# A blocked state scan on TensorE: two more products on all four quadrants, with copies that cross the partition halves

## The reference

```python
def step(s, inp):
    r_t, k_t, v_t, kk_t, a_t, w_t = inp
    sa = jnp.einsum("dbhij,dbhj->dbhi", s, kk_t)
    s = (s * w_t[..., None, :] - sa[..., :, None] * (kk_t * a_t)[..., None, :]
         + v_t[..., :, None] * k_t[..., None, :])
    y = jnp.einsum("dbhij,dbhj->dbhi", s, r_t) if readout else None
    return s, y
return lax.scan(step, state0, xs)
```

## Time and profile before

| what | value |
|---|---|
| median of three runs | 1297.73 us (1296.73 to 1299.86) |
| the profiled execution, its own time | 1300.72 us |
| its span, first to last instruction | 1298.9 us |
| PE busy | 1219.1 us (94%) |
| DVE busy | 540.9 us (42%) |
| ACT busy | 360.2 us (28%) |
| POOL busy | 115.3 us (9%) |
| mean granted TensorE clock | 0.982 |
| the scan's loop, steps 1 to 8 | 174.19 to about 368 us of the span |

### The profile page before, as it was taken

One profiled execution on the slowest core, in us unless ns is written; L12 is line 12 of the kernel. 1 busy time (PEld: TensorE's weight loads), 2 busy tenths in 40 slices (PEclk: granted clock), 3 DMA queues, 4 the chain that ended last, 5 costly groups with the idle time before them and its releaser, 6 DMA issues.

```text
span 1298.9 us, 23465 instructions
## 1 busy us (share of the span) xinstructions
PE 1219.1 (94%) x10171; PEld 855.6 (66%) x10171; DVE 540.9 (42%) x1110; ACT 360.2 (28%) x863; POOL 115.3 (9%) x135
## 2 busy tenths in 40 slices
PE   4999889898898999999989999999999979999996
PEld 1435777787777888888868887656678653343333
DVE  3158234446432999970030732575244140111113
ACT  3346144355421321111011211455431032111101
POOL 0004244334100001220000000000000000000000
PEclk9999889999998999999989999999999979999998
DMA  9700013322373334334343333211065539999991
GB/s 389 315 13 33 1 51 117 108 77 76 108 293 130 130 137 185 132 123 171 130 147 141 128 113 136 78 66 65 1 261 195 194 130 373 423 422 420 421 420 76
DMA packets 28038, 225.04 MB, mean 173 GB/s; under 512 B 3424, under 2 KB 6624, under 8 KB 7328
## 3 DMA queue, kind: packets, MB, share of 16 engines
q1 hardware_dynamic: 27536, 222.17, 43.9%
q0 software_dynamic: 256, 1.06, 0.2%
q10 hardware_dynamic: 144, 0.31, 0.1%
HBM read 220.38 MB, written 1.05 MB: 170 GB/s over the span
## 4 chain that ended last, share of the span: by engine, by line
PE 88%; DVE 4%; ACT 3%; issue 2%; DMA 2%; POOL 1%; DVEq 0%; SPq 0%; ACTq 0%
PE ps L738 37%; PE ps L1404 9%; PE ps L1198 6%; PE ps L886 5%; PE ps L1257 5%; PE ps L1455 4%; PE ps L1416 2%; PE ps L1303 2%; PE ps L1274 2%; PE ps L888 2%; PE ps L770 1%; PE ps L1381 1%; PE ps L865 1%; PE ps L1002 1%; PE ps L1288 1%
## 5 line engine op out<-in xcount | busy, mean ns | idle before, releaser
L738 PE MATMUL ps<-mem 128*128 128x256 f32 (+2 forms) x2032 | 499.3, 403 | 9.2 <-DVE mem L2232 4.2
L738 PEld LDWEIGHTS ps<-mem 128*128 128x128 f32 x2032 | 386.7, 192 | 112.2 <-issue 42.7
L2213 DVE SCALAR_TENSOR_TENSOR mem<-ps,mem 128x189 f32<-128x189 f32 (+2 forms) x352 | 148.3, 431 | 15.6 <-ACT mem L1754 4.7
L886 PE MATMUL ps<-mem 64*64 64x64 f32 (+1 forms) x2176 | 106.9, 239 | 19.9 <-DVE mem L2006 3.8
L886 PEld LDWEIGHTS ps<-mem 64*64 64x64 f32 x2176 | 87.9, 138 | 42.7 <-issue 20.7
L1404 PE MATMUL ps<-mem 128*34 128x512 f32 x512 | 112.8, 593 | 0.0
L888 PE MATMUL ps<-mem 64*64 64x64 f32 (+1 forms) x2176 | 105.3, 239 | 2.0 <-issue 1.9
L1516 ACT ACTIVATE mem<-ps 128x512 f32<-128x512 f32 (+4 forms) x110 | 68.4, 639 | 97.7 <-PE ps L888 70.7
L888 PEld LDWEIGHTS ps<-mem 64*64 64x64 f32 x2176 | 87.7, 138 | 2.5 <-issue 2.3
L1404 PEld LDWEIGHTS ps<-mem 128*34 128x34 f32 x512 | 29.9, 111 | 76.9 <-issue 76.8
L2429 DVE TENSOR_TENSOR mem<-ps,mem 128x512 f32<-128x512 f32 x32 | 22.2, 693 | 133.1 <-PE ps L1416 133.1
(11 more groups left out here) (285 smaller groups left out, 1289.2 us busy)
## 6 DMA issues: line engine op xcount, KB each, us to landing
mem<-experts SPq DMA_DIRECT2D x96, 1024.0 KB, 14.7
mem<-weights SPq DMA_DIRECT2D x44, 2048.0 KB, 8.5
mem<-late_ada SPq DMA_DIRECT2D x16, 1024.0 KB, 4.9
mem<-weights SPq DMA_DIRECT2D x3, 1536.0 KB, 6.8
mem<-tokens SPq DMA_DIRECT2D x1, 2048.0 KB, 7.9
mem<-mem SPq DMA_DIRECT2D x32, 64.0 KB, 2.5
mem<-consts SPq DMA_DIRECT2D x1, 1519.0 KB, 16.7
mem<-consts POOLq DMA_DIRECT2D x1, 776.0 KB, 5.2
```

What stands on the lines that cost most here:

```text
L738: last = mm(bank(j % banks)[:, 0:nn], w[:, kc, c * P:(c + 1) * P], rr(kc), start=kc == 0, stop=kc == KD - 1)
L886: mm(out[hp, 0, j], lhs[hp, 0, j], rhs[hp, 0, j], start=True, stop=True)
L2213: n(stt(out=o, in0=src[:, r0 + dy:r1 + dy, c0 + dx:c1 + dx], scalar=prm("ffn_conv", tap * 2 * NG + j), in1=o, op0=ALU.mult, op1=ALU.add))
```

## The change

Both products now cross for `d` 1, so the argument `crossed` is gone. Their results for `d` 1 then lie in the wrong half, and the copies out of PSUM carry them across: a copy that crosses reads one half and writes the other, and takes one instruction for each half. reads_kept becomes two instructions on ScalarE, the third gram two on VectorE, and X3's `d` 1 is split: ScalarE (`keep_solution`, after its copy of `d` 0) carries HIGH to LOW, and VectorE (a new `keep_solution`, counted as X3_crossed) LOW to HIGH. spread0 waits for X3_crossed too.

```diff
-                    for hp, to in ((LOW, HIGH), (HIGH, LOW)) if crossed else ((LOW, LOW), (HIGH, HIGH)):
+                    for hp, to in ((LOW, HIGH), (HIGH, LOW)):
...
-                product("turned", prep_bank(s, 1), RX[s % 2][:, :, :, FIRST], KX[s % 2][:, :, :, C:3 * C], 2 * C,
-                        crossed=False)
+                product("turned", prep_bank(s, 1), RX[s % 2][:, :, :, FIRST], KX[s % 2][:, :, :, C:3 * C], 2 * C)
...
-                solve(s, "X3", MTI, X0, crossed=False)
+                solve(s, "X3", MTI, X0)
...
-                    waits(s, "X3_kept", "reads_kept", "gram_kept")
+                    waits(s, "X3_kept", "X3_crossed", "reads_kept", "gram_kept")
...
-                keep(s, "reads_kept", GR[:, :, 2, :], made[:, 1, :, FIRST])
+                A(GR[LOW, :, 2, :], made[HIGH, 1, :, FIRST], ACT.Copy)
+                keep(s, "reads_kept", GR[HIGH, :, 2, :], made[LOW, 1, :, FIRST])
...
+            def keep_solution(s):
+                act.wait_ge(*turn("X3", s))
+                made = over_banks(CHAIN, width_of(s))
+                A(XB[:, 0, :, columns(s)], made[:, 0], ACT.Copy, scale=-1.0)
+                keep(s, "X3_kept", XB[LOW, 1, :, columns(s)], made[HIGH, 1], -1.0)
...
-                keep_factor(i - 1, "X3", -1.0)
+                keep_solution(i - 1)
...
-                tt(GR[:, :, 3, :], made[:, 1, :, SECOND], bc(grams[:, 0, :, FIRST], P, NJ, C), ALU.mult)\
-                    .then_inc(turns_of("gram_kept"), 1)
+                for rows, to in ((LOW, HIGH), (HIGH, LOW)):
+                    last = tt(GR[to, :, 3, :], made[rows, 1, :, SECOND], bc(grams[rows, 0, :, FIRST], 64, NJ, C), ALU.mult)
+                last.then_inc(turns_of("gram_kept"), 1)
...
+            def keep_solution(s):
+                dve.wait_ge(*turn("X3", s))
+                ts(XB[HIGH, 1, :, columns(s)], over_banks(CHAIN, width_of(s))[LOW, 1], -1.0, None, ALU.mult)\
+                    .then_inc(turns_of("X3_crossed"), 1)
...
                 if i >= READ_FROM:
                     keep_keys(i)
                 if i >= 1:
+                    keep_solution(i - 1)
                     keep_spread(i - 1, 0)
```

More of the change, by code:

```diff
@@ L528, in two_blocks @@
                 "chain_kept_by_scalar": (("X1_kept", "X3_kept", "for_state0", "for_state1", "state0"),) * 2,
-                "chain_kept_by_vector": (("X2_kept", "for_values0", "for_values1", "state1"),) * 2}
+                "chain_kept_by_vector": (("X2_kept", "X3_crossed", "for_values0", "for_values1", "state1"),) * 2}
         def turns_of(name):
@@ L879, in waits, with heads @@
                     pe.wait_ge(*turn(name, s))
-            def heads(b, width, lhs, rhs, crossed=True):
+            def heads(b, width, lhs, rhs):
                 out = over_banks(b, width)
@@ L886, in heads, with product @@
                         mm(out[hp, 0, j], lhs[hp, 0, j], rhs[hp, 0, j], start=True, stop=True)
-                    for hp, to in ((LOW, HIGH), (HIGH, LOW)) if crossed else ((LOW, LOW), (HIGH, HIGH)):
+                    for hp, to in ((LOW, HIGH), (HIGH, LOW)):
                         last = mm(out[to, 1, j], lhs[hp, 1, j], rhs[hp, 1, j], start=True, stop=True)
                 return last
-            def product(name, b, lhs, rhs, width=C, crossed=True):
-                heads(b, width, lhs, rhs, crossed).then_inc(turns_of(name), 1)
+            def product(name, b, lhs, rhs, width=C):
+                heads(b, width, lhs, rhs).then_inc(turns_of(name), 1)
             def removals(s):
@@ L972, in fourths_of_far, with solve @@
                 product("M4T", prep_bank(s, 0), B3, B4)
-            def solve(s, name, lhs, rhs, crossed=True):
-                product(name, CHAIN, lhs, rhs[:, :, :, columns(s)], width_of(s), crossed)
+            def solve(s, name, lhs, rhs):
+                product(name, CHAIN, lhs, rhs[:, :, :, columns(s)], width_of(s))
             def first_factor(s):
@@ L1559, in keep_far_square, with keep_factor @@
                 keep(s, "M2_kept", B3, over_banks(prep_bank(s, 0), C))
-            def keep_factor(s, name, scale=1.0):
-                act.wait_ge(*turn(name, s))
-                keep(s, name + "_kept", XB[:, :, :, columns(s)], over_banks(CHAIN, width_of(s)), scale)
+            def keep_factor(s):
+                act.wait_ge(*turn("X1", s))
+                keep(s, "X1_kept", XB[:, :, :, columns(s)], over_banks(CHAIN, width_of(s)))
+            def keep_solution(s):
[3 more added lines that the diff above has]
+                keep(s, "X3_kept", XB[LOW, 1, :, columns(s)], made[HIGH, 1], -1.0)
             def keep_spread(s, d):
@@ L1689, in _ @@
                     keep_mod(i - 2)
-                keep_factor(i - 1, "X1")
+                keep_factor(i - 1)
                 if i == STEPS:
@@ L2147, in _ @@
             bonus_term(3)
+            keep_solution(STEPS - 1)
             keep_spread(STEPS - 1, 0)
```

## The result

The changed kernel is slower: 1309.91 us, median of five runs (1307.78 to 1312.82), against 1299.86 us for the kernel before in the same comparison (five runs, 1296.73 to 1304.65). The ratio is 1.0064, 95% interval 1.0042 to 1.0087, or +8.3 us on 1299.86 (the two medians are 10.1 apart). The forecast was no change, 1298.0 us with a range from 1294.5 to 1301.5; the measured median lies above it.

A forecast was written before the change was run, and what follows sets the result against it. TensorE was taken to bound the kernel nearly everywhere, with added copies paying back its savings: turned -2.5 and X3 +2.8 gave +0.3 us, 1301.0 for the profiled execution and 1298.0 us for the median, range 1294.5 to 1301.5.

The forecast's parts named there:

- X3, chunks 0 to 2: -0.18 each: Q1 can't move; spread0 no longer waits for X3's copy and starts when Q1 ends; three times gives -0.54 us.
- turned part of chunk 7: After turned TensorE goes straight to the late piece; copies have the 4.78 us transfer's time, so the full 0.8 us is won.
- sum of +0.3: All terms on the profiled execution's 1300.7 us: turned -2.5 and X3 +2.8, together +0.3 us.
- rival 3: The clock falls in TensorE's added idle time: one fall 1300.4 us, two 1302.8 to 1304; chance 0.20, 0.12 above 1301.6.
- second stretch at clock 0.50 between 180 and 370 us: Listed sign that the forecast is wrong: another stretch of the scan at half clock.
- 1.1 to 1.3 us: Sign of being right: TensorE's idle time before removalsT of chunks 1 to 5, where it had been 0.64 us.
- 0.28 + 0.34: Added ScalarE and VectorE copies behind turned, chunks 0 to 4; against 0.80 us won, leaves -0.18 us each.
- X3, chunk 3 (step 4): +1.85: spread0 waits for VectorE's crossing copy behind `keep_keys`, until about 261.1 instead of 259.27: 1.85 us lost.
- Rival 2: Gaps without visible cause (1.86, 1.61 us) overlap the new waits: 1.8 to 3.5 us back, 1294.5 to 1296.2; chance 0.12.
- chunks 4 and 5: +0.45 each: X3's crossing copy behind `keep_keys`, ScalarE copies 0.49 us apart: spread0 starts about 285.40, not 284.94; 0.9 us for two.
- X3, chunk 6 (step 7): +0.6; chunk 7: 0: Step 7 loses 0.25 to 1.0 us, depending on the 1.61 us gap, middle taken; chunk 7 lies beside the transfer.
- two transfer waits at the scan's end: Waits for late weights, 4.78 and 7.41 us, move with the chain; X3 of chunk 7 is hidden beside the 7.41.

The follow-up runs named there:

- turned alone: Kernel before with only the product turned crossed and its copies in halves, X3 and its copy as before: 1303.93 us, ratio 1.0016.
- both orders: Changed kernel with VectorE's M4T_kept ahead of the grams and X3's crossing copy ahead of `keep_keys`: 1298.14 us, ratio 0.9973.
- burst: Kernel before plus 16 narrow and 16 wide thrown-away crossed products ahead of removalsT in step 2: 1330.62 us, one run.
- M4T_kept first: Kernel before, products untouched, with VectorE's M4T_kept ahead of the two grams: 1299.98 us, ratio 0.9995.

## Why the prediction was wrong

**What held.** The products: turned and X3 are as short as the crossed ones. "X3, chunks 0 to 2: -0.18 each" was measured as -0.18, -0.18, -0.18. The turned part of chunk 7 (-0.86 for -0.8) and the new waits before spread0 in steps 4 to 6 (1.92, 1.28 and 1.28 us) were as said, and the crossing copies are no longer than straight ones. At equal clock the sum of +0.3 became +1.3, inside the range.

**The step that failed: the clock, which the sum put at nothing, and rival 3, as I sized it.** The clock was worth 8.5 us in the profile and +7.2 by the fit; a "second stretch at clock 0.50 between 180 and 370 us" was the prediction's own sign of being wrong, and five came. "idle times of 1.86, 1.78 and 1.61 us in the scan passed at clock 1.00" was my argument against the clock, and I looked for a fall in step 4 alone, at most one more in step 7. I had myself lengthened the wait before removalsT to "1.1 to 1.3 us" in five steps and added three waits before spread0. Each for itself was, as expected, of a length that had passed before; I didn't ask what they do together. Measured, they were longer: up to 2.51 us. The runs show no length from which the clock falls: idle times of 1.88 (to 198.20) and 1.82 us (to 222.17) passed in the changed kernel's profile, and 1.28 didn't. The version with turned alone fell after 1.88 and 1.81. What changed is how often it happened: on average 64.9 us at half speed in a run, not 46.8. The rival's price for one fall, 2.4 us for 6.82 us at half speed, was fair (2.3 measured for 6.82 us, 1.5 to 1.6 for 3.41 us); the number, one or two, was wrong, and so was the chance of 0.12 above 1301.6.

**"0.28 + 0.34".** The spacings were taken from copies that all begin in the same half; the crossing ones didn't overlap. Measured per chunk for turned: +0.34 us in chunks 0 to 2, +0.66 in chunk 3, +0.38 in chunk 4, 0 in 5 and 6, -0.86 in 7. The sum is +1.2 where -2.5 was forecast. This is the largest error outside the clock, 3.7 us, and it lengthened the waits before removalsT (1.82 us in step 2, where 1.1 to 1.3 was expected). These terms are read from the changed kernel's trace; the level of turned alone, -3.8, doesn't match them, and only the missing gap named above explains a part of that.

**"X3, chunk 3 (step 4): +1.85".** Measured +1.03. Here rival 2 came true in part: the gap ahead of it was 0.90 us in place of 1.86. TensorE resumed 1.35 us after the end of the transfer of code (261.03), as elsewhere, but that transfer had begun 0.06 us before Q1 and not 0.85 after it; that it got ahead while TensorE waited and ran slowly is likely and not shown. **"chunks 4 and 5: +0.45 each"** became +0.82 each. ScalarE's copies start 0.61, 0.62 and 0.49 us apart, not 0.49 throughout:

```profile
289.51 0.60 ACT L1568 ACTIVATE mem<-ps 128x512 f32<-128x512 f32 x1 [3.46 <-PE ps L888]
290.12 1.71 ACT L1515 ACTIVATE mem<-ps 64x512 f32<-64x512 f32 x3
```

**"X3, chunk 6 (step 7): +0.6; chunk 7: 0".** Chunk 6 won 1.5 us instead, since the gap of 1.61 us was not there. Chunk 7 had lost 1.1 at its last spread, since its late piece had to wait 1.73 us for its transfer ahead of X3; by the last late piece, whose own wait is gone, the 1.1 were back, so the forecast of 0 holds to the end of the scan. Of the two transfer waits at the scan's end there is only one in the chain:

```profile
362.07 6.35 DMA mem<-late_ada
```

In all X3 came to +1.8 at the last spread and +0.7 at the last late piece, where +2.8 was forecast, and turned to +1.2 where -2.5 was. With the 0.2 around, the trace's terms sum to +2.1 at the last late piece, the level over all runs is +1.3 (plus or minus 0.8), and the forecast was +0.3: X3 too dear by 2.1 and turned too cheap by 3.7. That these errors partly cancel is luck.

**A slip in the chances.** Rival 2 was priced at 1294.5 to 1296.2, and yet a third of its chance was put below 1293.9. The result doesn't hang on it.

**What stays open.** Why turned alone gains 3.8 us at equal clock; why one idle time is followed by a slow stretch and a like one isn't; the share of the clock in a single run; and why several versions have two short slow stretches behind the scan, at about 355 and 375 us, where before and the changed kernel have none. The 0.40 us for a microsecond at half speed is a fit over runs, not an experiment; the profile agrees with it (8.5 us late for 20.5 us at half speed).

The best version is the changed kernel with both orders: 1298.14 us, ratio 0.9973 (0.9960 to 0.9986) to before. By the fit it would be 7.8 us faster at equal clock; more than half of that (4.4) goes to the clock.

## What to carry to other kernels

An edit that shortens TensorE's work and lengthens its waits by the same amount was not neutral here: price the idle time that it adds in every iteration, with the clock, not the longest one alone. An added copy goes behind whatever its consumer doesn't need, and moved copies are spaced by what they follow: look at which half the one ahead begins in. Before making narrow matmuls faster, count how many instructions they run through per microsecond.

## What the runs showed of the hardware that I had not expected

- Copies that begin in another half than the one ahead start when it has ended: 0.38 to 0.40 us apart on ScalarE and 0.42 to 0.46 on VectorE (256 elements), against 0.28 and 0.34.
- In the burst TensorE ran narrow matmuls no faster than its code arrived: 256 instructions in 3.73 us, where they need 1.9, with gaps of 1.64 us at every block.
- In the changed kernel's profile the granted clock fell to 0.50 five times in a scan of 190 us, for 3.41 to 6.83 us each, after idle times of 1.28 to 2.51 us. In the profile of before, whose idle times are mostly under 1 us, it didn't fall there; with M4T_kept first it fell three times, once after 0.83 us. So no single idle time tells whether the clock will fall, and only the average over many runs tells two kernels apart.
